# Two decoder blocks on one core: the final-norm weighting moved ahead of two low parts on GpSimd, one rounding moved into the norm stage, the rescaling of the residual two chunks later, a down-projection tile moved one place in the weight stream, and a sine sign moved to the mixing block

## The reference, cut to what matters

```python
for layer in range(2):                       # first_block
    h = h + (gated_deltanet | sliding_window_attention)(rmsnorm(h, norm_w))
    h = h + conv_gated_mlp(rmsnorm(h, ffn_norm_w[layer]), w_up, conv_w, conv_b, w_down)   # 1024 -> 2 x 2816 -> 1024
x = rmsnorm(h, final_norm_w)
# second_block
h = rms_norm(x, pre_mix_norm)
h_q, h_k, h_v, h_g, h_a, c_q, c_kv, k_pe = split(h @ w_in)
y_a = gla_branch(h_q, h_k, h_v, h_g, h_a, ...) @ w_o_gla
y_b = mla_branch(c_q, c_kv, k_pe, cos, sin, ...) @ w_o_mla      # rotary embedding with cos, sin of the positions
g_a, g_b = split(sigmoid(h @ w_gate + b_gate))
x = x + rms_norm((g_a * y_a + g_b * y_b) @ w_out, post_mix_norm)
x = x + rms_norm((silu(h2 @ w_gate) * (h2 @ w_up)) @ w_down, post_ffn_norm)   # h2 = rms_norm(x, pre_ffn_norm)
```

## Time and profile before

| | before |
|---|---|
| time, median of 3 runs | 1250.04 us (1249.17 to 1252.81) |
| the profiled execution | 1249.66 us, span of its trace 1247.8 us |
| TensorE busy | 1194.3 us, 96% of the span |
| GpSimd busy | 879.8 us, 71% |
| VectorE busy | 714.5 us, 57% |
| ScalarE busy | 705.1 us, 57% |
| low parts on GpSimd (L167) | 363, 2435 ns each |
| roundings on ScalarE (L163) | 364, 1055 ns each |

### The profile page before, as it was taken

How to read it: one execution, slowest core, us unless ns; L and a number is a source line. 1 busy time by engine, 2 the same in 40 slices (tenths; PEclk the granted TensorE clock), 3 DMA queues, 4 the chain that set the end, 5 groups by cost and what they waited for, 6 DMA issues and landing times.

```text
span 1247.8 us, 23366 instructions
## 1 busy us (share of the span) xinstructions
PE 1194.3 (96%) x8148; PEld 1078.2 (86%) x8148; DVE 714.5 (57%) x1513; ACT 705.1 (57%) x1319; POOL 879.8 (71%) x371
## 2 busy tenths in 40 slices
PE   8999899898999999999999999799999999999996
PEld 6988898777999998888999998778788887999996
DVE  4657667465766667446666666167344634444444
ACT  7667677455565556656655555565366445444442
POOL 5836643257888886726888896888778465988882
PEclk9999999999999999999999999899999999999999
DMA  7687522235866665524566664566556344666650
GB/s 274 198 162 168 157 90 85 69 105 166 241 197 188 191 194 166 170 67 128 168 194 189 194 199 143 168 187 186 168 165 223 102 131 139 187 187 192 182 162 34
DMA packets 61064, 203.27 MB, mean 163 GB/s; under 512 B 6320, under 2 KB 12720, under 8 KB 60864
## 3 DMA queue, kind: packets, MB, share of 16 engines
q1 hardware_dynamic: 53280, 192.96, 50.8%
q10 hardware_dynamic: 7712, 9.32, 3.7%
HBM read 198.07 MB, written 4.19 MB: 162 GB/s over the span
## 4 chain that ended last, share of the span: by engine, by line
PE 33%; issue 32%; POOL 31%; DVE 2%; DMA 1%; ACT 0%; POOLq 0%; SPq 0%; DVEq 0%; ACTq 0%
POOL wlo L167 31%; PE bank L180 8%; PE bank L181 8%; PE bank L182 8%; PE solve L182 2%; PE solve L181 2%; PE solve L180 2%; DMA raw<-in_stream 1%; PE bank L1718 0%; PE bank L1719 0%; DVE resid L2139 0%; POOL scr L2302 0%; DVE scr L2134 0%; PE bank L1644 0%; PE bank L1635 0%
## 5 line engine op out<-in xcount | busy, mean ns | idle before, releaser
L167 POOL TENSOR_TENSOR wlo<-raw,whi 128x1024 fp32r<-128x1024 f32 x363 | 874.7, 2435 | 345.5 <-ACT whi L163 343.9
L163 ACT ACTIVATE whi<-raw 128x1024 fp32r<-128x1024 f32 x364 | 381.1, 1055 | 138.1 <-PE bank L182 124.5
L180 PE MATMUL bank<-xhi,whi 128*128 128x256 f32 x936 | 271.3, 290 | 7.7 <-POOL wlo L167 4.0
L181 PE MATMUL bank<-xlo,whi 128*128 128x256 f32 x936 | 265.9, 284 | 0.0
L182 PE MATMUL bank<-xhi,wlo 128*128 128x256 f32 x936 | 265.7, 284 | 0.0
L180 PEld LDWEIGHTS bank<-xhi,whi 128*128 128x128 f32 x936 | 180.4, 193 | 11.2 <-POOL wlo L167 4.3
L180 PE MATMUL bank<-whi,xhi 128*128 128x512 f32 (+2 forms) x456 | 180.7, 396 | 8.1 <-issue 4.4
L181 PEld LDWEIGHTS bank<-xlo,whi 128*128 128x128 f32 x936 | 180.5, 193 | 1.2
L182 PEld LDWEIGHTS bank<-xhi,wlo 128*128 128x128 f32 x936 | 180.3, 193 | 0.0
L181 PE MATMUL bank<-wlo,xhi 128*128 128x512 f32 (+2 forms) x456 | 175.9, 386 | 0.0
L182 PE MATMUL bank<-whi,xlo 128*128 128x512 f32 (+2 forms) x456 | 175.8, 386 | 0.0
(11 more groups left out here) (414 smaller groups left out, 1729.8 us busy)
## 6 DMA issues: line engine op xcount, KB each, us to landing
raw<-in_stream SPq DMA_DIRECT2D x364, 512.0 KB, 3.7
band_scratch<-band ACTq DMA_DIRECT2D x1, 3072.0 KB, 35.2
area<-band_scratch ACTq DMA_DIRECT2D x2, 1024.0 KB, 8.9
resid<-in_x SPq DMA_DIRECT2D x2, 512.0 KB, 6.4
scr<-in_row_b_gate ACTq DMA_DIRECT2D x1, 1024.0 KB, 4.6
out<-resid SPq DMA_DIRECT2D x4, 256.0 KB, 2.0
tab<-in_tabs ACTq DMA_DIRECT2D x1, 640.0 KB, 10.7
area<-in_row_final ACTq DMA_DIRECT2D x1, 512.0 KB, 5.5
```

Of the source, the lines that this page charges most:

```text
L163: act.activation(whi[:, n.s, :], raw[:, n.s, :], ACT.Copy).then_inc(hi_ready, 1)
L167: pool.tensor_tensor(wlo[:, n.s, :], raw[:, n.s, :], whi[:, n.s, :].bitcast(F32), ALU.subtract).then_inc(lo_ready, 1)
L180: nc.tensor.matmul(out_ap, a_hi, b_hi, start=start, stop=False)
L181: nc.tensor.matmul(out_ap, a_hi, b_lo, start=False, stop=False)
```

## The change

It has five parts:

- **GpSimd's list.** The weighting stood behind the low part of unit 221; it stands behind that of unit 220. The loop over the ring ends one round earlier and five low parts are written out.
- **`raw_act`.** In the norm stages ahead of ffn0, the attention, ffn1 and the mixing block, two roundings stood behind the whole stage. The first now stands behind the third square. In the mixing block, the first square of the weighted rows follows it, and the other three stand behind the second rounding.
- **Rescaled rows.** The four instructions of L1802 and the DMA of the gates' bias stood ahead of the `cq` and `ckv` copies; they stand behind chunk gv0. Three roundings (units 223 to 225) stood behind the wait for the root; they stand ahead of it.
- **Order of the weight stream.** In every feed-forward block the down unit of tile 17 stood ahead of gate and value of tile 20; it stands behind them. The lists of TensorE and ScalarE follow; ScalarE's loop has a round less, with six tiles written out.
- **Sine sign.** VectorE's multiplication moves from the end of the attention to the mixing block, ahead of `KP`.

```diff
--- before.py
+++ after.py
@@ -357,7 +357,7 @@
 
-        def raw_act(act, key, norm, junk=scr):
+        def raw_act(act, key, norm, last, junk=scr, beside=None):
             def square_of(n):
@@ -368,11 +368,16 @@
             square_of(2)
+            if key != "ffn2":
+                refill(act, last - 1)
+            if beside:
+                beside()
             for k in (4, 5):
...
                 hi_of(act, key, 0, k)
+            refill(act, last)
 
@@ -451,9 +456,9 @@
             if what == "down":
-                return unit(b + (3 * j + 6 if j < NF - 4 else 2 * NF + j), 2 * i)
+                return unit(b + (3 * j + 6 if j < NF - 5 else 3 * j + 8 if j == NF - 5 else 2 * NF + j), 2 * i)
             half = 0 if what == "gate" else 1
-            return unit(b + half + (2 * j if j < 2 else 3 * j - 2 if j < NF - 1 else 3 * j - 3), 2 * i)
+            return unit(b + half + (2 * j if j < 2 else 3 * j - 2 if j < NF - 2 else 3 * j - 3), 2 * i)
 
@@ -484,8 +489,8 @@
             up(19, 0)
+            up(20, 0)
             down(17, 0)
-            up(20, 0)
             up(21, 0)
@@ -528,14 +533,18 @@
             refill(act, ffn_unit(f, 1, 0, "down"))
-            with act.Fori(0, 4) as i:
+            with act.Fori(0, 3) as i:
                 for j in (4, 5, 6, 7):
...
                     refill(act, ffn_unit(f, j - 2, i, "down"))
-            for j in (20, 21):
+            for j in (16, 17, 18, 19, 20, 21):
                 tile_of(j, 0)
...
                     beside(j)
+                if j < 19:
+                    refill(act, ffn_unit(f, j - 2, 0, "down"))
+                elif j == 20:
+                    refill(act, ffn_unit(f, 17, 0, "down"))
             refill(act, ffn_unit(f, NF - 4, 0, "down"))
@@ -1558,8 +1567,6 @@
             rope_angles(dve)
-            dve.wait_ge(IN.sin, 1)
-            dve.tensor_scalar(sinT[:], sinT[:], colv("rope_sign"), None, ALU.mult).then_inc(IN.rope, 1)
 
@@ -1789,24 +1796,22 @@
 
-            raw_act(act, "mix", "final", junk)
-            refill(act, BASE["cq"] - 2)
-            refill(act, BASE["cq"] - 1)
-            act.dma_start(W_A2[0:16, :], w_a2).then_inc(MX.w_a2, 16)
-            for n, (t, h, cols) in enumerate(BANKS):
+            def weighted_square(n):
+                t, h, cols = BANKS[n]
                 act.wait_ge(RS.weighted, n + 1)
                 square(act, "mix", n, scr[:, t, cols], junk2[:, t, cols])
+
+            raw_act(act, "mix", "final", BASE["cq"] - 1, junk, lambda: weighted_square(0))
+            for n in (1, 2, 3):
+                weighted_square(n)
+            act.dma_start(W_A2[0:16, :], w_a2).then_inc(MX.w_a2, 16)
             r = root_of("mix")
+            for k in range(3):
+                refill(act, BASE["cq"] + k)
             act.wait_ge(RS.root, RAW["mix"] + 1)
-            for t, h, cols in BANKS:
-                act.activation(resid[:, t, cols], scr[:, t, cols], ACT.Copy,
-                               scale=root_of("final")[:, t:t + 1]).then_inc(rescaled, 1)
-            act.wait_ge(rescaled, 4)
-            act.dma_start(scr[:].rearrange("p t c -> p (t c)"),
-                          rows["b_gate"].broadcast_to([P, 2 * D])).then_inc(MX.row_gate, 16)
             for name, n, dst, b0, width in (("cq", 4, CQ, 0, QL), ("ckv", 2, CKV, 2, KVL)):
-                for k in range(n - 1):
-                    refill(act, BASE[name] + k)
+                if name == "ckv":
+                    refill(act, BASE[name])
                 for t in range(NT):
@@ -1844,6 +1849,12 @@
             chunk(1)
+            for t, h, cols in BANKS:
+                act.activation(resid[:, t, cols], scr[:, t, cols], ACT.Copy,
+                               scale=root_of("final")[:, t:t + 1]).then_inc(rescaled, 1)
+            act.wait_ge(rescaled, 4)
+            act.dma_start(scr[:].rearrange("p t c -> p (t c)"),
+                          rows["b_gate"].broadcast_to([P, 2 * D])).then_inc(MX.row_gate, 16)
             chunk(2)
@@ -1975,8 +1985,9 @@
             dve.tensor_tensor(GK, GK, LX, ALU.mult).then_inc(MX.kdec, 1)
+            dve.wait_ge(IN.sin, 2)
+            dve.tensor_scalar(sinT[:], sinT[:], colv("rope_sign"), None, ALU.mult).then_inc(IN.rope, 1)
             dve.wait_ge(IN.rope, 1)
-            dve.wait_ge(IN.sin, 2)
             dve.memset(KP[64:P, 0], 0.0)
@@ -2289,18 +2300,23 @@
         def _(pool):
-            mid = BASE["cq"] // RING + 1
+            ahead = BASE["cq"] + RING - 2
+            own = ahead // RING
             pool.wait_ge(lo_ready, 1)
...
                 rest_of_unit(pool, unit(k))
-            with pool.Fori(1, mid) as i:
+            with pool.Fori(1, own) as i:
                 for k in range(RING):
                     rest_of_unit(pool, unit(k, i))
+            for k in range(own * RING, ahead):
+                rest_of_unit(pool, unit(k))
             pool.wait_ge(SW.row_final, 16)
...
                 pool.tensor_tensor(scr[:, t, cols], resid[:, t, cols], row_final[:, cols], ALU.mult).then_inc(RS.weighted, 1)
-            with pool.Fori(mid, UNITS // RING) as i:
+            for k in range(ahead, (own + 1) * RING):
+                rest_of_unit(pool, unit(k))
+            with pool.Fori(own + 1, UNITS // RING) as i:
                 for k in range(RING):
@@ -2313,21 +2329,15 @@
             delta_act(act)
-            raw_act(act, "ffn0", "ffn0")
-            refill(act, BASE["ffn0"] - 2)
-            refill(act, BASE["ffn0"] - 1)
+            raw_act(act, "ffn0", "ffn0", BASE["ffn0"] - 1)
             copy_root(act, "ffn0", ps[1][:, 0:SEQ])
             ffn_act(act, 0, True, lambda tile: swa_load(act, tile))
-            raw_act(act, "b", "b")
-            refill(act, BASE["kv"] - 2)
-            refill(act, BASE["kv"] - 1)
+            raw_act(act, "b", "b", BASE["kv"] - 1)
             for k in range(KD):
...
             swa_act(act)
-            raw_act(act, "ffn1", "ffn1")
-            refill(act, BASE["ffn1"] - 2)
-            refill(act, BASE["ffn1"] - 1)
+            raw_act(act, "ffn1", "ffn1", BASE["ffn1"] - 1)
             copy_root(act, "ffn1", ps[1][:, 0:SEQ])
@@ -2405,16 +2415,12 @@
 
-def d_rest(d):
-    return [d[j] for j in range(NF - 4, NF)]
-
-
 def ffn_units(up_gate, up_val, down):
...
     for j in range(3, NF):
-        order += [g[j], v[j]] + ([d[j - 2]] if j < NF - 2 else [])
-    return np.stack(order + d_rest(d))
+        order += [g[j], v[j]] + ([] if j == NF - 3 else [d[j - 3]] if j == NF - 2 else [d[j - 3], d[j - 2]] if j == NF - 1 else [d[j - 2]])
+    return np.stack(order + [d[NF - 2], d[NF - 1]])
 
```

More of the change, by code:

```diff
@@ L1937, in block2_act @@
                 square(act, "post_mix", n, ACC[t][h], junk[:, t, cols])
-            raw_act(act, "ffn2", "ffn2")
-            refill(act, BASE["ffn2"] - 1)
+            raw_act(act, "ffn2", "ffn2", BASE["ffn2"] - 1)
             copy_root(act, "ffn2", ps[1][:, 0:SEQ])
```

## The result

The changed kernel takes 1233.16 us (median of 4 runs, 1231.58 to 1234.24); the kernel before, with one more run beside it, 1249.61. The ratio is 0.9863, 95% interval 0.9841 to 0.9886: 17.1 us less, and between 14.2 and 19.9. The forecast was 1236.5 with a range from 1233.5 to 1241.0; the sign and the places were right, the gain was 3.3 us larger than forecast, and the median lies 0.3 us under the range. The profiled execution took 1232.24 us, its span 1230.5.

A forecast was written before the change was run, and what follows sets the result against it. The prediction took TensorE, busy 96% of the span, plus its pauses as the bound. Gains of 10.6 + 2.0 + 0.9 = 13.5 us from 1249.66 gave 1236.2, forecast as 1236.5 us, range 1233.5 to 1241.

The forecast's parts named there:

- Start of the mixing block: Both TensorE pauses for low parts of weights go: 7.4 us of pause and 3.2 of half clock, 10.6 us gained.
- Start of ffn1: TensorE's wait for the second addition to the residual goes once the sine multiplication moves away: 2.0 us gained.
- Rescaled rows and sine in the mixing block: Rescaling two chunks later and the sine multiplication in VectorE's chain (slack 9.6 us) were each costed at nothing.
- my upper 2.4: Mixing block: the moved sine multiplication was to take from 0.4 to 2.4 us in VectorE's chain.
- The rival of a slower chain on VectorE: Mixing block: VectorE's small instructions each wait out a low part and the chain becomes the bound; full price 1267, chance 0.02.
- Roundings elsewhere: Ahead of ffn0, attention and ffn1, TensorE doesn't wait for weights, so rounding behind the third square brings nothing.
- Ends of the feed-forward blocks: Waits for the last tile's `flo` shrink by 0.6 us in ffn0 and 0.3 in ffn1: 0.9 us gained.
- The laid out order: Last feed-forward tiles, timed tile by tile against GpSimd's boundaries: `flo` 0.6 us earlier in ffn0, 0.3 in ffn1.
- Moves with GpSimd's boundaries: Ends of feed-forward blocks: VectorE instructions meeting a running low part end when it ends, so `flo` follows GpSimd's boundaries.
- its bounds, 3.3 and a loss of 2.4: Ends of ffn0 and ffn1: 3.3 us gained if both pauses go; 2.4 lost each if an instruction misses a boundary.
- the 0.3 that the forecast added for the median: Whole kernel: 1236.2 became 1236.5, because the profiled execution lay 0.4 us below the median.
- a rival, both `flo` pauses gone: Ends of ffn0 and ffn1 lose their pauses whole: 10.6 + 2.1 + 3.3 = 16.0 us, 1234.0; chance 0.10.

The follow-up runs named there:

- e1: Kernel before with the parts at the norm stages and mixing block, without weight stream and sine moves: 1240.35 us, ratio 0.9911.
- e5: Changed kernel with GpSimd's old order, both roundings behind the norm stages as before, weighted squares together behind them: 1238.53 us, ratio 0.9905 to the kernel before.
- e7: Changed kernel with only GpSimd's old order back and the four weighted squares together behind the second rounding: 1235.04 us, ratio 0.9880.
- e8: Changed kernel with both roundings behind the norm stages again, weighted squares together behind them, GpSimd's new order kept: 1233.88 us, ratio 0.9881.
- e6: Changed kernel with rescaling and bias DMA back ahead of the cq copies and roundings of units 223 to 225 behind them: 1239.75 us, ratio 0.9919.
- e10: Changed kernel with rescaling and bias DMA back behind the wait for the root, roundings of units 223 to 225 left ahead of it: 1232.64 us, ratio 0.9877.
- e2: Kernel before with the sine sign multiplication moved alone: 1248.66 us, ratio 0.9985.
- e3: Kernel before with the new order of the weight stream alone: 1249.21 us, ratio 0.9993.
- e4: The changed kernel measured again, with more rounds, against the kernel before: 1233.58 us, ratio 0.9869.
- e12: The changed kernel measured once more, beside a version with the weight stream one step further: 1231.89 us, ratio 0.9864.

## Why the prediction was right in its places, and where it was short

- **Start of the mixing block, 10.6 us:** right. Alone (e1) 10.64 in the trace and 11.1 in the time. The two pauses have separate causes, as worked out: the first comes back only if GpSimd's order and the early rounding are both undone (e5, e7, e8), the second if the roundings of 223 to 225 stand behind both the root and the rescaling (e6; roundings ahead of the root are enough, e10; the late rescaling alone was not run).
- **Start of ffn1, 2.0 us:** 2.07 in the trace, 1.9 in the time (e2).
- **Rescaled rows and sine in the mixing block, nothing:** right (e10; mixing to ffn2 is 256.1 us in every trace). The sine took 2.50 us there, a little over my upper 2.4. The rival of a slower chain on VectorE did not come: the chain ended at 849.5 and the scan did not wait.
- **Roundings elsewhere, nothing:** wrong by 0.4 us. I looked only for waits for weights. In the attention TensorE waits for ScalarE's copies (L1491), and ScalarE had one rounding less to do there; that wait went from 1.49 to 1.26 us. The other 0.2 is a gap too short for the table of waits: the first product of L1408 starts 0.31 us behind the product before it, and 0.48 in e2 and e8, which lack the early rounding.
- **Ends of the feed-forward blocks, 0.9 us:** this is the step that failed, by its size. Forecast were 0.6 + 0.3, measured 1.0 + 1.1 = 2.1 (e3). The laid out order took GpSimd's boundaries nearly as they were; but they had moved too. Counted from the first broadcast, the last `flo` of ffn0 ended at 177.4 us, 0.3 behind a low part that ended at 177.1; in the changed kernel and in e3 it ended at 176.4, 0.3 behind one that ended at 176.1. That is the 1.0 us. Why the low parts came earlier (ScalarE's roundings, which the stream moved, are ahead of them) was not tested. "Moves with GpSimd's boundaries" was the right mechanism, and a layout by hand of which side of a boundary each instruction falls on was worth no more than its bounds, 3.3 and a loss of 2.4.
- **The sum.** With 0.4 and 1.2 more it is 15.2 us, and the traces give just that behind the first broadcast. From the profiled execution, and with the 0.3 that the forecast added for the median, it would have been 1234.8 us, inside the range; so these terms are about half of the 3.3 us. The times give 17.1, 16.4 and 17.0 (from the ratios of the changed kernel, e4 and e12), each with 2 to 3 us on either side. The 1 to 2 us between are in none of these traces, but each execution has its granted clock, averaged over its span, on record. Both traces of the kernel before have 0.990. Of its 41 executions that ran beside the experiments 19 have that, and take 1248.3 us on average; the other 22 have 0.982 to 0.989 and take 1250.8. The 14 executions of the changed kernel take 1233.1. That is 15.2 us against the 19 and 16.5 against all 41. So the executions of the kernel before spent more time at half clock than its traces show. Where in the span they did is open, and with it whether this belongs to the pauses that the change removes. Of the four traces with both old pauses at the mixing block, e2 had 1.0 us more of half clock behind them and e3 1.5 us more behind the pause at ffn1, and the two of before neither. The part ahead of ffn0 gives no sign of it: the first broadcast is from 303.5 to 306.4 in these four and from 303.0 to 307.4 in the ten others.
- **The range.** Its lower end was the sum for both `flo` pauses gone, less 0.5. The forecast started from one execution; the two traces of the kernel before are 2.3 us apart ahead of ffn0 alone, and the half clock behind a pause changes too. That should have made the range at least 2 us wider. That the median lies only 0.3 us under it is partly luck: the range had its lower end there for a rival, both `flo` pauses gone, that did not come.

## What to carry to other kernels

When TensorE waits for a prepared operand, follow the preparing engines' lists back to the instruction that is in front of it without need: here a rounding stood behind a root and a rescaling that it didn't use, and a weighting stood in front of a low part. Two edits that each make the same operand early enough pay once; undo them one by one before keeping both. And price a pause at more than its length: what it takes from the clock behind it changes from one execution to the next.

## What the runs showed of the hardware

- A pause of 2.13 us was followed by a stretch at half clock (0.50 in 576 to 578 us) in one trace, and by none in three others with the same pause at the same place; behind one pause of 3.44 us the loss was 2.6 us (e5), behind one of 3.31 it was 1.6 (e6).
- Code that is the same in all 14 traces, up to the first transpose of the first feed-forward norm, took 292.8 to 297.2 us. In the first two, the granted clock was below 1.00 in different stretches (0.89 in 230 to 245 and 0.72 in 285 to 290 us before; 0.93 in 100 to 150 and 0.89 in 270 to 285 after), and a wait of 3.35 us for VectorE (L1289, L1298 in the changed kernel) was 1.71 in the other. In the two traces of before and the three of the changed kernel everything between the first and the last broadcast repeated to 0.1 us.
- A VectorE instruction on 128 x 2 values in SBUF took 1.85 us while GpSimd made a low part and 0.16 us while it was idle (L1963 in the changed kernel and in e6). That is the exclusive lock that the Trainium skill states (SBUF — State Buffer, "SBUF: two separate sides"); both measurements agree with it. The first row of the chain in the earlier trace rows, L250, which the prediction names beside the rule for two inputs, has only one tensor as input. It ended at 825.35, with the low part that ended at 825.32; so it too waited, but it is no case of two inputs.
